# Turning attention probabilities with rounded products instead of float32 transposes, in a hybrid encoder layer

## The reference

```python
def _window_attention(q, k, v, sink):
    ...
    s = jnp.einsum('bnqhgd,bnkhd->bnhgqk', qb, kb) * (HEAD_DIM ** -0.5)
    ...
    s = jnp.where(valid[None, :, None, None], s, -jnp.inf)
    ...
    m = jnp.maximum(jnp.max(s, axis=-1, keepdims=True), sk)
    p = jnp.exp(s - m)
    denom = jnp.sum(p, axis=-1, keepdims=True) + jnp.exp(sk - m)
    o = jnp.einsum('bnhgqk,bnkhd->bnqhgd', p / denom, vb)
    return o.reshape(B, S, N_Q_HEADS * HEAD_DIM).astype(q.dtype)
```

## Time and profile before

| what | value |
| --- | --- |
| median of 3 runs | 1052.65 us (1051.58 to 1054.05) |
| profiled execution, its own time | 1050.59 us |
| its span | 1048.8 us |
| mean granted TensorE clock | 0.995 |
| PE busy | 1014.9 us, 97% of the span |
| DVE busy | 686.7 us, 65% |
| POOL busy | 617.0 us, 59% |
| ACT busy | 473.1 us, 45% |

### The profile page before, as it was taken

One profiled execution on the slowest core, in us unless ns is written; L12 is line 12 of the kernel. 1 busy time (PEld: TensorE's weight loads), 2 busy tenths in 40 slices (PEclk: granted clock), 3 DMA queues, 4 the chain that ended last, 5 costly groups with the idle time before them and its releaser, 6 DMA issues. The chain is left out here.

```text
span 1048.8 us, 12973 instructions
## 1 busy us (share of the span) xinstructions
PE 1014.9 (97%) x4642; PEld 838.3 (80%) x4642; DVE 686.7 (65%) x781; ACT 473.1 (45%) x694; POOL 617.0 (59%) x374
## 2 busy tenths in 40 slices
PE   8999999999999999999979999999999999999996
PEld 6788788888888888877757888878888878888885
DVE  5746665204656653667996878868788588839755
ACT  3154445212455455474727484665746751102022
POOL 4762524455452432534587999999999834475223
PEclk9999999999999999999999999999999999999999
DMA  8343332575233211426233534344343689837012
GB/s 324 120 162 120 110 110 86 175 239 182 101 130 110 77 45 51 141 101 217 82 119 108 149 98 141 101 139 133 100 151 91 211 304 331 309 111 298 1 59 102
DMA packets 63541, 150.50 MB, mean 143 GB/s; under 512 B 6784, under 2 KB 7168, under 8 KB 63360
## 3 DMA queue, kind: packets, MB, share of 16 engines
q1 hardware_dynamic: 54848, 127.69, 36.9%
q10 hardware_dynamic: 8640, 22.11, 5.4%
HBM read 108.88 MB, written 40.89 MB: 143 GB/s over the span
## 5 line engine op out<-in xcount | busy, mean ns | idle before, releaser
L682 POOL TENSOR_SCALAR w_hi<-raw 128x1024 fp32r<-128x1024 f32 (+1 forms) x46 | 57.6, 1252 | 272.7 <-PE proj L818 218.3
L818 PE MATMUL proj<-xt_hi,w_hi 128*128 128x512 f32 x480 | 194.1, 404 | 2.3 <-DVE xt_lo L1526 1.1
L820 PE MATMUL proj<-xt_hi,w_lo 128*128 128x512 f32 x480 | 188.1, 392 | 0.0
L819 PE MATMUL proj<-xt_lo,w_hi 128*128 128x512 f32 x480 | 187.9, 391 | 0.0
L717 POOL TENSOR_TENSOR w_lo<-raw,w_hi 128x512 fp32r<-128x512 f32 x66 | 129.9, 1971 | 8.1 <-ACT w_hi L1156 3.7
L685 POOL TENSOR_TENSOR w_lo<-raw,w_hi 128x1024 fp32r<-128x1024 f32 (+1 forms) x46 | 123.4, 2682 | 3.8
L820 PEld LDWEIGHTS proj<-xt_hi,w_lo 128*128 128x128 f32 x480 | 90.2, 188 | 19.9
L818 PEld LDWEIGHTS proj<-xt_hi,w_hi 128*128 128x128 f32 x480 | 90.4, 188 | 19.0 <-DVE xt_lo L1526 2.3
L819 PEld LDWEIGHTS proj<-xt_lo,w_hi 128*128 128x128 f32 x480 | 90.5, 189 | 14.1
L1005 PE MATMUL proj<-xt_hi,w_hi 128*128 128x512 f32 x224 | 89.1, 398 | 8.3 <-DVE stage_out L1529 3.5
L1009 PE MATMUL proj<-xt_lo,w_hi 128*128 128x512 f32 x224 | 88.2, 394 | 0.0
(11 more groups left out here) (195 smaller groups left out, 2487.5 us busy)
## 6 DMA issues: line engine op xcount, KB each, us to landing
raw<-stream SPq DMA_DIRECT2D x52, 512.0 KB, 4.3
presum_a<-stream SPq DMA_DIRECT2D x42, 256.0 KB, 2.9
sums<-presum_a SPq DMA_DIRECT2D x42, 256.0 KB, 2.0
raw<-sums SPq DMA_DIRECT2D x38, 256.0 KB, 2.7
spill<-part ACTq DMA_DIRECT2D x16, 512.0 KB, 2.9
merges<-stage_out ACTq DMA_DIRECT2D x32, 256.0 KB, 2.7
raw<-stream SPq DMA_DIRECT2D x31, 256.0 KB, 2.7
raw_half<-stream SPq DMA_DIRECT2D x21, 256.0 KB, 2.7
```

Of the source, the lines that this page charges most:

```text
L682: nc.gpsimd.tensor_scalar(hi, raw[:, raw_slot, cols], 1.0, 0.0, ALU.mult, ALU.add)\
L818: begun = nc.tensor.matmul(bank, wh, mov_hi, start=first, stop=False)
L819: nc.tensor.matmul(bank, wh, mov_lo, start=False, stop=False)
L820: return begun, nc.tensor.matmul(bank, wl, mov_hi, start=False, stop=last)
```

## The change

`normalize` no longer writes `probs` in place. ACT writes the normalised probabilities rounded to fp32r into `probs_hi`. DVE gets one more instruction for each block, `probs_low`: (probs times the reciprocal) minus probs_hi, rounded, into `probs_lo`; it now gives probs_ready. PE turns each key block by two fp32r products with a unit matrix in fp32r, `unity`: first probs_hi with the bank opened, then probs_lo added. pt_ps, pt_hi and pt_lo stay as they were.

`unity` is copied once from `ident` by ACT. probs_hi and probs_lo take the same bytes as `part`, so in the second group ACT waits until the stores of the first have landed.

```diff
+            with ExitStack() as plain:
+                probs_hi = allot(plain, "probs_hi", [P, 2, HALF], f32r)
+                probs_lo = allot(plain, "probs_lo", [P, 2, HALF], f32r)
             part = allot(stage, "part", [P, 2, SEQ])
             presum_b = allot(stage, "presum_b", [P, HALF])
+            unity = allot(stage, "unity", [P, P], f32r)
...
                 for i in range(nk):
                     at = (3 - nk + i) * P
-                    last = nc.tensor.transpose(pt_ps[:, i * P:(i + 1) * P], probs[:, n % 2, at:at + P],
-                                               ident)
+                    for p in (probs_hi, probs_lo):
+                        last = nc.tensor.matmul(pt_ps[:, i * P:(i + 1) * P], p[:, n % 2, at:at + P], unity[:, :],
+                                                start=p is probs_hi and i == 0, stop=p is probs_lo,
+                                                skip_group_check=True)
                 last.then_inc(pt_done, 1)
...
                 act.wait_ge(rdenom_done, m + n + 1)
-                nc.scalar.activation(probs[:, n % 2, c0:3 * P], probs[:, n % 2, c0:3 * P], ACT.Identity,
-                                     scale=rdenom[:, 0:1]).then_inc(probs_ready, 1)
+                nc.scalar.activation(probs_hi[:, n % 2, c0:3 * P], probs[:, n % 2, c0:3 * P], ACT.Identity,
+                                     scale=rdenom[:, 0:1]).then_inc(probs_hi_done, 1)
...
+            act.wait_ge(table_landed, 32)
+            copy(unity[:, :], ident)
             rope_hi(k_hi, 1, 0)
...
                 exponentials(g * HEADS * NB, 0)
+                if g:
+                    for i in range(2):
+                        act.wait_ge(spilled[i], 16 * (1 + KT // 2 * g))
                 normalize(g * HEADS * NB, 0)
...
+            def probs_low(m, n):
+
+                c0 = (3 - len(key_blocks(n))) * P
+                dve.wait_ge(probs_hi_done, m + n + 1)
+                stt(probs_lo[:, n % 2, c0:3 * P], probs[:, n % 2, c0:3 * P], rdenom[:, 0:1],
+                    probs_hi[:, n % 2, c0:3 * P].bitcast(f32), ALU.mult, ALU.subtract)\
+                    .then_inc(probs_ready, 1)
...
                         last.then_inc(pt_split, 1)
+                    if n < NB:
+                        probs_low(m, n)
                     if n == 2:
                         silu(g, h)
...
                         if more:
                             denominators(m + NB, 0)
+                            probs_low(m + NB, 0)
                         attention_lo(g, h, 1)
```

More of the change, by code:

```diff
@@ L419, in encoder_layer @@
         rdenom_done = sem("rdenom_done")
+        probs_hi_done = sem("probs_hi_done")
         tap_done = sem("tap_done")
@@ L1715, in _ @@
                 denominators(g * HEADS * NB, 0)
+                probs_low(g * HEADS * NB, 0)
                 with dve.Fori(0, HEADS - 1) as h:
```

## The result

The changed kernel takes 1087.16 us (median of 4 runs, 1085.53 to 1088.42) against 1052.41 before (4 runs): a ratio of 1.0327, 95% interval 1.0309 to 1.0346, +34.8 us. Slower was forecast, but by 22 us, and 1087 lies above the stated range, which ended at 1083. The profiled execution has a span of 1085.4 us.

What follows compares the result with a forecast made beforehand. PE, busy 97%, was taken as the bound. 19.9 us of PE work plus 2 of waits gave 21.9, on the runs' median of 1052.65 us 1074.6, say 1075; the 8-in-10 range was 1066 to 1083.

Steps and rivals of the forecast that it cites:

- PE's work: 176 float32 turns on PE become two fp32r products each, 0.111 to 0.224 us a key block: +19.9 us.
- rival 1: Weight loads hide in part when six short products run in a row, 0.085 us each: +14 us, 1067; chance 9%.
- rival 3: A short fp32r product not paired with a longer one takes more than one pass: +59 us, 1114; chance 2%.
- rival 4: Weight loads hide wholly, 0.058 us a product, +1.1 us, and waits don't grow: 1053 to 1054; chance 3%.
- The waits: PE's added waiting from DVE's new instruction and longer chain: 0.3 us in six loop heads, say 2; bounds 0 and +15.6.
- The price: DVE's new instruction taken at 0.56 us, pt_lo's time for 384 columns from the bank; bounds 0.5 and 0.95.
- The place: At the head boundary, q_lo ends 0.49 us ahead of the next head's scores; 0.2 us of wait expected there.
- The cover: Turns of blocks 1, 3, 5, 7 and 0 have a 1.4 us slice more in front: no added wait.
- the wait at block 2: PE's waits before block 2's turn stay at 4.7 us, with 0.1 us added for the loop heads.
- Rival 2: DVE's chain becomes the bound, POOL slowing probs_low to 0.95 us, at each turn behind scores: +35.5 us, 1088; chance 6%.
- The sign named for this rival: PE waiting in most turns behind scores would show the forecast wrong and point to Rival 2.

Runs made afterwards that it cites:

- two_hi: Changed kernel with each key block turned by two products, both of probs_hi, and no new DVE instruction: 1067.89 us, ratio 1.0156 to the kernel before.
- one_hi: Changed kernel with PE turning probs_hi alone, one product a key block, and no new DVE instruction: 1052.29 us, ratio 1.0003 to the kernel before.
- The quiet pair: Kernel before and changed kernel, both with POOL's work in the attention cut to 8 columns an instruction: 1045.48 and 1065.07 us.
- short_low: Changed kernel with PE turning probs_hi twice and DVE's probs_lo cut to its first 8 columns, still waited for: 1070.89 us, ratio 1.0174.
- one_wait: Changed kernel with one product a key block, of probs_hi; DVE still makes probs_lo and the turn waits for it: 1078.67 us, ratio 1.0255.

## Why the prediction was wrong

**PE's work: right.** 0.111 a turn and 0.112 a product were forecast, 0.67 us for six products; measured 0.67. Over all turns of two_hi the six hold PE for 0.670 us in the median and the four of a short block for 0.445, against 0.328 and 0.219 before: 48 x 0.342 + 16 x 0.226 = 20.0 us, forecast 19.9. one_hi shows the same by its time. Rivals 1, 3 and 4 fall with it. The 81 ns that the Trainium skill, "TensorE: Matmul & The Clock Gate", section "Back-to-back issue gap", gives for a product of 128 columns isn't met here: it is 112.

**The waits: the step that failed.** "So 0.3 us in each of the six loop heads, 1.8 us, say 2." Measured it is 34.8 - 20.0 = 14.8. The step took DVE's new instruction to be short and covered nearly everywhere; it meets POOL's instructions instead, and what stands behind it in DVE's queue reaches PE late. The distances between the turns, summed over the heads, tell where, the changed kernel (span 1085.4) against two_hi (1066.1), which has the same work on PE. They come from the starts of the 64 turns in the two timelines:

| stretch | over two_hi, us |
| --- | --- |
| block 7 to the next head's block 0 (7 times) | 6.7 |
| block 0 to 1 (8) | 7.0 |
| block 1 to 2 (8) | 3.1 |
| block 2 to 5 | 0.9 |
| block 5 to 7 | 2.1 |

The sum is 19.8 and not 14.8 for two reasons. The turns of two_hi stand only 16.0 us further apart than those before, for 20.0 us of work, so it has filled some 4 us of old waits. Most of the other 1 us comes from the profiled executions, whose spans lie 36.6 us apart where the medians lie 34.8. 13.7 of the 19.8 us lie at the boundary of the heads, for which 0.2 us a head, at the scores, had been put down. The tile's view has the price (shortest, median and longest in ns, first and last start in us):

```profile
L1541 DVE SCALAR_TENSOR_TENSOR probs_lo<-probs,rdenom,probs_hi x64: 474/618/2465, 56.5 to 418.1; 128x384 fp32r<-128x384 f32 x48, 128x256 fp32r<-128x256 f32 x16
```

Three things in that step were off:

- The price. "I take 0.56": undisturbed it is 0.62 for 384 columns, and the mean of the 64 is 0.83. The upper bound, 0.95, was no bound either; the longest is 2.47. Taking the smallest of the near rows, when the earlier trace rows showed the same kind of instruction at 1.15, was a choice against the row that it is nearest to: both read two operands in SBUF.
- The place. The contention was weighed for the new instruction alone. At the boundary DVE has q_lo, at_lo, the new instruction and at_lo again, four that POOL can stretch, in one queue ahead of the mask of block 1. The earlier trace rows gave q_lo 0.49 us of lead over the scores; a presum beside it takes 1.1.
- The cover. Blocks 1 and 7 had "a slice of six products (1.4 us) more in front of their turn. Nothing." The way from block 0's turn to block 1's is where the loss is largest, 7.0 us. In two heads DVE starts the mask of block 1 2.6 us after the turn of block 0, 1.6 and 1.8 later than in two_hi; in two others the turn of block 1 itself starts 1.3 us late. A cover of 1.4 us on PE doesn't hold against what POOL can add to several instructions of DVE's queue.

Of the wait at block 2, "its 4.7 us stay" holds only with DVE's instruction: in two_hi 1.5 us are left. The quiet pair shows that PE's term was right for a kernel without POOL: +19.6, forecast 19.9, with nothing left for the waits. Rival 2 named the cause that came (POOL slowing the instruction), but its size, 1088, is luck. It put the whole loss at the 24 turns behind scores and counted 0.65 us for each, though it set the instruction alone at 0.95; with 1.05 it would have been 1098. Of these turns, over two_hi, block 2's are 2.0 us later in all eight heads together and block 6's 1.3 us; block 4's are not late at all. The sign named for this rival, that PE waits in most turns behind scores, did show, in 16 of 24, but most of the loss lies elsewhere. In rival 1, PE would arrive 0.30 us later and not 0.26 (five key blocks of 0.059); that moves nothing.

**The rule.** The ends in that timeline fit together like shifts. q_lo starts at 127.42 beside a presum that ends at 128.69, and ends 1.09 us after it; the next presum starts at 128.78 and ends 1.15 us after q_lo; at_lo starts at 129.70 and ends 0.55 us after that presum; at 134.93 at_lo starts again, 0.11 us behind the weight split, and ends 0.55 us after the split's end at 137.25. Each is held until the other engine's instruction is done. In the changed kernel 34 of the new instructions, q_lo and at_lo are stretched by more than 0.1 us, and every one of them does this: they end behind the end of an instruction of POOL by 0.27 to 0.28 us with 256 columns, 0.41 to 0.42 with 384, 0.53 to 0.55 with 512 and 1.08 with 1024; in short_low it is 0.01 to 0.03 us with 8. The row is of this kind too: at_lo ends at 158.84, 0.53 behind POOL's 158.31. pt_lo, which has one operand in the bank and one in SBUF, never takes more than 0.56 us in any run. The Trainium skill, "SBUF — State Buffer", section "Who interferes with whom", says just that of a DVE instruction with two SBUF inputs and a GpSimd instruction that reads SBUF: the second one waits until the first has finished. By this rule, with which the trace agrees, a meeting isn't priced by a ratio such as 1.15 to 0.68, but by what is left of POOL's instruction, here up to 2.3 us. It spoke against this change, and the prediction left it out.

## What to carry to other kernels

Where rows show that another engine holds up instructions of the same kind, price a new instruction by those rows, and price with it everything behind it in its queue: 64 instructions of 0.48 or 0.62 us, with room on their engine, cost 15 us here, most of it at the boundary of the heads. Two short products in place of one float32 turn cost twice its time. A product of 128 fp32r columns is held at 0.112 us by something other than its stream: the second product of an undelayed turn starts 0.06 us after the first, and only the later ones are 0.11 apart. To find which of length, wait or neighbour costs, cut each alone. Here the wait without the length cost 2 to 3 us, the length without the wait about 5, and with POOL quiet the whole change cost no more than PE's own work.

## What the runs showed of the hardware that was not expected

The first product of a turn that starts late costs PE about 0.1 us beyond the delay. In the turn of block 0 above PE starts at 135.13 and the second product at 135.29, 0.16 later; in the unhindered one at 115.26 the second starts 0.06 later. In the changed kernel 28 of the 64 turns begin so, just those that start late by 0.015 us or more. The six products of such a turn hold PE for 0.77 us instead of 0.67. In one_wait there are 40, in two_hi and before 6, the turns of block 2 (0.08 us more in two_hi, and with the three float32 turns before only 0.03: 0.36 instead of 0.33). 22 more of them at 0.1 make some 2 us of the loss, an estimate from these counts.

Both engines lose when they meet: beside the presums q_lo takes 2.36 us instead of 1.23, and the presum behind it takes 2.15 where the one ahead took 1.29. With the presums gone the kernel before is 4 us faster too.
